# Normalizing attention probabilities in two VectorE instructions, and turning the first four key tiles behind the first

## The reference, cut to what matters

```python
for i in range(seq // Q_BLOCK):                       # Q_BLOCK = 128, seq = 1024
    q_lo, q_hi = i * Q_BLOCK, (i + 1) * Q_BLOCK
    qb, kb, vb = q[:, q_lo:q_hi], k[:, :q_hi], v[:, :q_hi]
    s = jnp.einsum('bqhd,bkhd->bhqk', qb, kb).astype(jnp.float32) * scale
    ...
    p = jax.nn.softmax(jnp.where(mask, s, NEG_INF), axis=-1).astype(v.dtype)
    outs.append(jnp.einsum('bhqk,bkhd->bqhd', p, vb))
```

## Time and profile before

| what | value |
|---|---|
| median of 3 runs | 1484.33 us (1483.67 to 1485.74) |
| the profiled execution | 1482.75 us, its span 1480.6 us |
| PE busy in the span | 1439.2 us (97%) |
| DVE busy in the span | 1002.7 us (68%) |
| granted TensorE clock | 1.0 of full speed |
| low halves (L861), first to last start | fox 214.0 to 339.1 us, mla 428.5 to 552.5 us of the span |

### The profile page before, as it was taken

The page is one execution under the profiler, slowest core; times in us unless marked ns, Lnnn a source line. Parts: engine busy times, 40 slices in busy tenths (PEclk is TensorE's granted clock), DMA queues, the critical chain, the costliest instruction groups (busy, mean ns, idle before and its releaser), DMA issues.

```text
span 1480.6 us, 18895 instructions
## 1 busy us (share of the span) xinstructions
PE 1439.2 (97%) x7090; PEld 1206.3 (81%) x7090; DVE 1002.7 (68%) x1378; ACT 651.7 (44%) x1054; POOL 127.1 (9%) x104
## 2 busy tenths in 40 slices
PE   7999999999999999998999999999999999999998
PEld 6999987778877777886788888888888888888887
DVE  5212366765676767757845778878778877679786
ACT  6230235554435543226522355555555555444332
POOL 1000141001420003102200000000000000000000
PEclk9999999999999999999999999999999999999999
DMA  7101231132121014226762212222222221891222
GB/s 262 62 0 75 64 93 41 39 108 76 36 67 52 29 37 112 54 75 215 232 239 85 91 52 85 86 85 86 86 81 77 85 86 56 318 386 64 86 78 79
DMA packets 130085, 148.93 MB, mean 101 GB/s; under 512 B 11018, under 2 KB 94909, under 8 KB 129725
## 3 DMA queue, kind: packets, MB, share of 16 engines
q1 hardware_dynamic: 129808, 147.67, 30.3%
q10 hardware_dynamic: 189, 0.08, 0.0%
HBM read 110.83 MB, written 36.31 MB: 99 GB/s over the span
## 4 chain that ended last, share of the span: by engine, by line
PE 53%; DVE 6%; issue 1%; ACT 1%; POOL 0%; DMA 0%; DVEq 0%; ACTq 0%
PE ps L1894 28%; PE ps L2201 5%; PE ps L2203 5%; PE ps L2202 5%; PE ps L2773 2%; PE ps L2771 2%; PE ps L2772 2%; PE ps L540 2%; PE ps L2290 1%; DVE plain_arena L2297 1%; PE ps L2803 0%; DVE plain_arena L2561 0%; PE ps L1530 0%; DVE plain_arena L1042 0%; ACT plain_arena L2273 0%
## 5 line engine op out<-in xcount | busy, mean ns | idle before, releaser
L1894 PE MATMUL ps<-split_arena 128*128 128x512 f32 x1320 | 306.8, 389 | 0.0
L540 PE MATMUL ps<-split_arena 128*128 128x512 f32 x1152 | 290.2, 399 | 3.9 <-PEq L1122 2.1
L1894 PEld LDWEIGHTS ps<-split_arena 128*128 128x128 f32 x1320 | 247.4, 188 | 51.5 <-issue 0.3
L540 PEld LDWEIGHTS ps<-split_arena 128*128 128x128 f32 x1152 | 208.3, 188 | 45.1 <-issue 5.5
L2077 ACT ACTIVATE down_ops<-down_all 128x1024 fp32r<-128x1024 f32 x77 | 81.7, 1062 | 115.4 <-PE ps L2203 115.4
L1894 PE MATMUL ps<-up_b,split_arena 128*128 128x512 f32 x528 | 126.5, 389 | 0.0
L2096 DVE TENSOR_TENSOR down_ops<-down_all,down_ops 128x1024 fp32r<-128x1024 f32 x77 | 94.2, 1224 | 46.3 <-ACT down_ops L2077 46.1
L2201 PE MATMUL ps<-down_ops 128*128 128x512 f32 x308 | 119.9, 389 | 0.5 <-DVE down_ops L2096 0.5
L2202 PE MATMUL ps<-down_ops 128*128 128x512 f32 x308 | 119.8, 389 | 0.0
L2203 PE MATMUL ps<-down_ops 128*128 128x512 f32 x308 | 119.8, 389 | 0.0
L1894 PEld LDWEIGHTS ps<-up_b,split_arena 128*128 128x128 f32 x528 | 99.1, 188 | 20.6
(11 more groups left out here) (359 smaller groups left out, 2507.9 us busy)
## 6 DMA issues: line engine op xcount, KB each, us to landing
plain_arena<-in_w_in SPq DMA_DIRECT2D x24, 512.0 KB, 4.2
scr_gate<-plain_arena SPq DMA_DIRECT2D x48, 256.0 KB, 2.0
plain_arena<-scr_gate SPq DMA_DIRECT2D x24, 512.0 KB, 4.4
plain_arena<-in_w_up SPq DMA_DIRECT2D x22, 512.0 KB, 5.2
up_raw<-in_w_up SPq DMA_DIRECT2D x22, 512.0 KB, 4.8
scr_act<-plain_arena SPq DMA_DIRECT2D x22, 512.0 KB, 2.7
down_all<-scr_act SPq DMA_DIRECT2D x18, 512.0 KB, 8.7
down_all<-in_w_down SPq DMA_DIRECT2D x18, 512.0 KB, 10.2
```

The costliest lines, as they stand in the source:

```text
L540: mm = nc.tensor.matmul(m.ps[:, self.banks[half], :], w[:, k, :], src[:, k, h * BANK:(h + 1) * BANK], start=(j == 0), stop=(j == self.PER_ ...
L1894: mm = nc.tensor.matmul(o, self.w[j][w][:, k, :], self.h[j][k][h], start=(j in self.OPENS and k == 0 and n == 0), stop=(k == self.HK - 1 a ...
```

## The change

`norm` multiplies in pieces of up to 512 columns (four key tiles). So steps with five to eight key tiles issue two multiplications instead of one, and each adds one to the semaphore `normed`. `normed_before(s)` counts how many such increments precede step s. PE waits before the first fill for the first piece of step s, and before the last fill for all of them.

```diff
     @staticmethod
+    def normed_before(s):
+        return s // TT * (TT + PAIRS) + s % TT + max(0, s % TT - PAIRS)
...
-            pe.wait_ge(self.normed, s + 1)
+            pe.wait_ge(self.normed, self.normed_before(s) + 1)
             *first, last = self.fills_of("p", s)
             for f in first:
                 self.turn(pe, f)
 
             if first:
                 self.fill.tensor(pe, ATT_FILL[i])
+            pe.wait_ge(self.normed, self.normed_before(s + 1))
             self.turn(pe, last)
...
-        V.tensor_scalar(self.p_buf[b][:, 0:keys], self.p_buf[b][:, 0:keys], self.rinv[:, b:b + 1], None, ALU.mult).then_inc(self.normed, 1)
+        for a in range(0, keys, BANK):
+            part = self.p_buf[b][:, a:min(keys, a + BANK)]
+            V.tensor_scalar(part, part, self.rinv[:, b:b + 1], None, ALU.mult).then_inc(self.normed, 1)
```

## The result

Over 14 runs each the changed kernel has a median of 1487.41 us (1484.86 to 1490.39), the kernel before 1484.97 us (1482.99 to 1489.15). The ratio is 1.0016, with a 95% interval of 1.0009 to 1.0024: between 1.3 and 3.6 us slower. The forecast was 1485.5 us, 1.2 us more than before, in a range of 1483.6 to 1487.6.

A forecast was written before the change was run, and what follows sets the result against it. PE, busy 1439.2 of 1480.6 us, plus its few holes was taken as the bound. Shorter waits 0, added DVE instructions 8 x 0.15 = 1.2 us, added PE waits 0: 1484.33 + 1.2 = 1485.5 us, range 1483.6 to 1487.6.

The forecast's parts named there:

- No first fill waits for the norm, so the shorter wait is worth 0: First fills of 32 steps: released by PE's own place or an earlier fill's low half, never the norm; worth 0.
- the first rival: First piece frees PE sooner at 8 places, 0.20 us each, 1.6 us less, 1482.7 us; chance 0.07.
- Eight exposed places, 0.15 us each: i = 6 in 4 heads of 2 attentions: the added DVE instruction delays PE 0.15 us each, 1.2 us more.
- In odd heads 0.14 and not 0.25 us: Norm at i = 6, fox head 1: two pieces take 0.86 us, 0.14 more, rather than 0.97, 0.25 more.
- 24 places covered by DVE's idle time: Steps i = 4, 5, 7: the extra 0.15 to 0.25 us lies beside DVE idle time of 0.56 us or more.
- A satisfied wait costs PE 0: Added PE wait before the last fill: taken as 0, read from 0.01 us at 262.88.
- One of the prediction's own signs of being wrong: Last fills of i = 4, 5 or 7: the prediction is wrong if a hole opens on PE there.
- It moves along rigidly, nothing gives it back: Chain behind PE at i = 6: the delay of 0.15 us counts once, not twice, and isn't recovered.
- Sum: All terms together: 8 x 0.15 = 1.2 us more, median 1485.5 us.
- a dearer split in odd heads: Norm at i = 6: 0.15 us in even heads, 0.25 in odd, making the forecast's cost 1.6 us.
- a hole in PE at i = 6: Added wait's upper end: 0.16 us in each of 8 exposed places, 1.3 us, making the cost 2.9.
- the spread of runs: Whole kernel: three runs spread by 2.1 us, so the median may lie 1 us to either side.

The follow-up runs named there:

- e5: Kernel before, norm whole; at i = 6 the low half of step 5's first fill is made ahead of the norm: ratio 0.9986.
- e9: e10 with only the norm of i = 6 in two pieces, PE's wait for the second ahead of the gate matmuls: ratio 0.9945, median 1477.21 us.
- e10: Kernel before, norm whole; low halves ahead of the norm at i = 6 (two, last head one) and of the maximum at i = 7 (one, not last head): 0.9962.
- e1: Changed kernel, but PE waits for all pieces before the first fill, with no added wait before the last: ratio 1.0004 to the kernel before.
- e3: Changed kernel with the wait for the last piece moved ahead of the gate matmuls: ratio 1.0002 to the kernel before.
- e4: e1 with the norm of i = 4 to 7 in pieces of 256 columns: offset +3.10 us to the kernel before, one run.
- e2: Kernel before, norm whole, plus a wait before the last fill on what has long been reached: ratio 1.0006.
- e11: Kernel before, norm whole, one added wait before the last fill, behind the low half's wait instead of ahead: offset 0.00 us, one run.
- e7: Kernel before, norm whole, two added satisfied waits before the last fill (norm and reciprocal): offset +0.60 us, one run.

## Why the prediction was right, and where its size was off

- *No first fill waits for the norm, so the shorter wait is worth 0.* Right. After the change no PE wait got shorter. e5 shows what PE waits for at i = 6. e9 against e10 shows that the same split is worth 0.2 us a place as soon as the norm is what PE waits for, the 0.20 us that the first rival had worked out for a place. That rival had the mechanism and the price; only its premise failed.
- *Eight exposed places, 0.15 us each.* Right in place, 0.13 us in size: 1.06 us in e1 and 1.03 in e3 for 1.2. e4's triple dose gave 0.38 a place.
- *In odd heads 0.14 and not 0.25 us.* Right: 0.72 became 0.85 us in fox head 1. By the Trainium skill (VectorE: DVE Perf Modes, section "Two Vector instructions with no wait between them") the second piece isn't held. The two pieces' 0.82 us, where 0.49 and the prediction's estimate of 0.42 laid end to end make 0.91, agree.
- *24 places covered by DVE's idle time.* Right: no jump there, even with four pieces in e4.
- *A satisfied wait costs PE 0.* Wrong, the term that was mis-sized. It was read at 262.88, where PE was behind with its own work. At the 12 last fills where it really waits, the added wait costs 0.065 us. With the small losses at i = 2 and the gains at i = 0 this is 0.46 us in e2. One of the prediction's own signs of being wrong showed here: PE's idle time grew at the last fills of i = 7, and the 1.2 us before last fills, which were to stay, became 1.4. The prediction also said that such a wait at i = 6 stands in front of one that comes later anyway, and took this as the reason for 0. That is where it costs: the added wait takes the place on the weight load, and the late one moves to the separate instruction (e11).
- *It moves along rigidly, nothing gives it back.* True of the pieces, as e1 and e4 show. The 0.06 us that PE gains at each i = 0 in the changed kernel come from the added wait there (e11), which the prediction had at 0 as well.
- *Sum.* 1.2 us forecast; 1.06 + 0.46 = 1.52 by the parts, 1.55 to 1.61 by the whole. The first comparison's 2.4 us (1.3 to 3.6) holds these. What lies above them isn't located; the granted clock, which moves single runs by 2 us and more, is the likely place, not a shown one. That the measured median, 1487.41 us, still lies in the range is in part luck: it is 0.2 us under the upper end, and that end had been set for a dearer split in odd heads, a hole in PE at i = 6 and the spread of runs, not for this.

## What to carry to other kernels

A producer's last instruction isn't what a consumer waits for just because it writes the operand: list every semaphore of the waiting instruction, buffer returns above all, and see which is made last in the producer's own order. Split an instruction only where it is that last one, and put the work that others need sooner ahead of it first; here the order was worth 4.4 us, and only then was the split worth 1.3 instead of costing 1.1. Put an added wait ahead of work that covers it (e3), or put the wait that comes late first in the text, so that it is the one on the instruction itself (e11).

## What the runs showed of the hardware

A late semaphore on PE that sits in a separate semaphore instruction in front of the weight load costs 0.05 to 0.08 us against one on the load itself, at 12 last fills each of e2, e7 and the changed kernel and, at 0.05 to 0.07, at i = 2 in e11. A satisfied one in the separate instruction costs nothing there (e11, last fills), nor does one ahead of other matmuls (e3). An added instruction on VectorE cost 0.13 us in a row of its instructions that don't wait (e1 and, with three added, e4). The mean granted clock of one and the same kernel varied from run to run: e1's twelve runs took 1483.2 to 1484.8 us in the seven at 1.0 and 1486.0 to 1488.3 us in the five at 0.998 and 0.999. Matmul-by-matmul offsets resolve 0.03 us beside it.
